# Decoder step on one core: sample states on 96 rows, ten tiles of the second output unit in the norm's banks, fourteen cache copies moved

## The chip, the cores and the metric

The program runs on one core of a Trainium2 chip. The metric is the device time of one execution in microseconds. TensorE (PE) multiplies matrices, VectorE (DVE) and ScalarE (ACT) work on tiles, GpSimd (POOL) adds and issues some transfers, SyncE (SP) issues most transfers. The eight banks of the accumulator memory have the names bSA, bSB, bO, bZ, bT0, bT1, bPA and bPB; the profile writes bT for bT0 and bT1.

## The reference, cut to what matters

One layer of a decoder serves a prompt of 512 tokens and 8 samples of 4 new tokens, 544 columns in all, with a model width of 2048. One input projection feeds gated linear attention (4 heads, key width 128, value width 256) and dilated softmax attention (8 heads, with a cache of 2048 positions for each sample). An output projection, a residual, a norm and a convolutional feed-forward part follow. Among the outputs are each sample's new linear-attention state and its shifted cache.

```python
# linear attention, block by block; a sample's four tokens are one block
s_new = s * exp(tot)[..., None] + einsum('bhsd,bhsv->bhdv', k_to_end, v)
# cache of a sample: old rows shifted by the four new ones
k_buf = concatenate([cache_k, k_new], axis=1)[:, -2048:]
# output projection and residual
h = x + concatenate([o_a, o_b], axis=-1) @ w_out
```

## The kernel before, in words

All matrices are kept transposed: features on the 128 rows, the 544 tokens on columns, in two halves of 272. Work on TensorE comes in *units*: 128 columns of a weight matrix against all 16 feature tiles of the input. A float32 weight is split by ScalarE into a rounded high part (`hi`, line 1043) and by VectorE into the rest (`lo`, line 1423), the input likewise, and `mm3` (lines 626 to 628) adds three fp32r products per tile and half. A unit is so 96 products of 272 columns. Two weight buffers take turns. `project(x, c)` does one half of unit c in bank bPA or bPB; it waits until both parts of the weights are there (`lo_done`) and until VectorE has read the bank's last result (`half_read`).

The engines run in their own program order and meet at semaphores. The stages are: softmax attention of 8 heads (to about 462 us), linear attention of 4 heads (to about 803), output projection of 16 units (to about 997), feed-forward. Units of the next head are projected between the steps of the present one.

**A linear-attention head** (`gla_head`, three times in a loop and once written out) turns keys and values into rows (ScalarE copies them from the banks: `KN`, `GVN`), adds up the chunk states, makes the outputs, and updates the 8 samples' states. For that update VectorE multiplies the 32 sample rows of the values by a 0/1 mask per sample (`masked(i)`, line 1601, four samples at a time, twice a head), and TensorE multiplies the keys with each masked copy in float32 (`sample_adds(i)`, line 911, four products of 256 columns, once ahead of the norm's sums in line 916 and once later). VectorE adds the result to the decayed states (line 1645). The norm over a head's 256 values goes through banks bZ and bT0: TensorE sums squares into them, VectorE reads them (lines 1650, 1651), ScalarE takes a root, VectorE inverts (line 1654) and multiplies (lines 1661 to 1665) into the last tiles of the residual.

**The output projection.** In the last head the first output unit starts early: `first_out` works its tiles in the order 8 to 15, then 0 to 7, both halves at a time. The two tiles that the last head makes come last (`READY` = 14), when `mixed_high` (line 1108) and `mixed_low` (line 1556) have split them. The second unit follows with `project`, then a loop of seven rounds does two units each. Behind each unit VectorE adds the residual (line 1692), ScalarE squares and scales (lines 1192, 1194) and splits the weights of the unit after the next, and GpSimd stores the tile (line 2113).

**SP's queue** in the looped heads holds, behind each of six weight loads, two or three copies of the samples' value cache (`copy_cache`, 584 KB each). In the output stage it holds, for each of twelve units, a weight load, a residual tile (as soon as the store that uses its buffer has landed) and three or four copies of the key cache. Ahead of the fourth unit's load it waits for the last head's sample states to be stored.

Of the kernel before, what the change touches and what calls it, by code (L numbers as in the profile page):

```python
# [15 lines left out]
F32 = mybir.dt.float32  # L16
# [78 lines left out]
def build(nc, A, O):  # L95
# [57 lines left out]
    SMK, o = place("causal_sample", [SAMP, SAMP], F32, o)  # L153
    RM, o = place("row_of_sample", [SAMP, NB], F32, o)

# [31 lines left out]
    ET, o = place("decay_total", [P, 16], F32, o)  # L187
    VM, o = place("v_masked", [SAMP, 4, DV], F32, o)
    OS, o = place("outputs_sample", [P, 2, SAMP], F32, o)
    assert o <= o_reset  # L190
    AT = KD
    OR = KD


# [97 lines left out]
    or_done, or_turned, os_done = sem("or_done"), sem("or_turned"), sem("os_done")  # L292
    vm_done, us_done, ss_done = sem("vm_done"), sem("us_done"), sem("ss_done")
    sq2_done, gsum_done, gms_done, gsqrt_done = sem("sq2_done"), sem("gsum_done"), sem("gms_done"), sem("gsqrt_done")
# [85 lines left out]
    H, ACTS = (nc.dram_tensor(n, s, F32, kind="Internal").ap() for n, s in (("hidden", [KT, P, T]), ("activations", [FT, P, T])))  # L380
    MIX_ORDER, READY = [*range(8, KT), *range(8)], KT - 2
    POFF = [0, 128, 384, 768]
# [5 lines left out]
    def _(sp):  # L388
# [87 lines left out]
        for it in range(GH - 1):  # L476
            cols = [it * P + (C_QA + P), it * P + (C_KA + P), it * DV + (C_VA + DV),
                    it * DV + (C_VA + DV + P), it * DV + (C_GA + DV), it * DV + (C_GA + DV + P)]
            j = 0
            for i, col in enumerate(cols):  # L480
                load_unit(unit_of(col), flat, U_GLA + 6 + i, it, 6)
                for _ in range(3 if i < 2 else 2):
                    copy_cache(1, it, j)
                    j += 1
            assert j == COPIES

# [19 lines left out]
        for it in range(3):  # L506
            for i in range(4):
                load_unit(w_cols(w_out, it * 4 * P + (3 + i) * P), raw3, U_OUT + 3 + i, it, 4)
                load_x(it * 4 + (2 + i), 2 + i, it)
                for j in range([0, 4, 8, 11][i], [4, 8, 11, 14][i]):  # L510
                    copy_cache(0, it, j)
        load_unit(w_cols(w_out, 15 * P), raw3, U_OUT + 15)
# [110 lines left out]
    def _(pe):  # L623
# [12 lines left out]
        def steps(x, c, lo, hi, it=None, k=0):  # L636

            if lo == 0 and x == 0:
                pe.wait_ge(lo_done, at(c + 1, it, k))
            if lo == 0 and c >= 1:  # L640
                pe.wait_ge(half_read, at(2 * c + x - 1, it, 2 * k))
            s = c % 2
            for kt in range(lo, hi):
                w = slice(kt * P, (kt + 1) * P)
                t = slice(x * HALF, (x + 1) * HALF)
                ins = mm3(PJ[x][:, 0:HALF], WH[s][:, w], WL[s][:, w], XH[:, kt, t], XL[:, kt, t], kt == 0, kt == KT - 1)
            if hi == KT:
                ins.then_inc(half_done, 1)
# [170 lines left out]
        def gla_head(it, c, last):  # L819
# [28 lines left out]
            pe.wait_ge(ke_done, n(1, 1))  # L848
            pe.wait_ge(gv_done, n(4, 2))
            for j in range(4):  # L850
                turn(T0[:, j * P:(j + 1) * P], g0[:, 1, j * P:(j + 1) * P], P)
            turn(T1[0:SAMP, 0:P], g0[:, 1, SEQ:T], P).then_inc(kn_turned, 1)
            project(1, u + 1, it, 6)
            pe.wait_ge(kn_done, n(2, 2))
            pe.wait_ge(half_read, at(2 * u + 2, it, 12))
            turn_v(g1[:, 0])
            project(0, u + 2, it, 6)

            pe.wait_ge(gv_done, n(4, 4))
            for ch in range(NCH):  # L860
# [46 lines left out]
            def sample_adds(i):  # L907
                pe.wait_ge(vm_done, n(2, i + 1))
                for b in range(4):
                    dst = [T1, BO][b // 2]  # L910
                    ins = pe.matmul(dst[:, (b % 2) * DV:(b % 2 + 1) * DV], KN[0:SAMP, 4, :], VM[:, b, :], start=True, stop=True)
                ins.then_inc(us_done, 1)
# [18 lines left out]


        first_out(READY, KT)
        project(0, U_OUT + 1)
        project(1, U_OUT + 1)
        for it in range(7):
            for i in range(2):
                project(0, U_OUT + 2 + i, it, 2)
                project(1, U_OUT + 2 + i, it, 2)

# [92 lines left out]
    def _(act):  # L1033
# [76 lines left out]
        def gla_head(it, c, last):  # L1110
# [25 lines left out]
            def v_rows(w):  # L1136
                act.wait_ge(gv_turned, n(2, w + 1))
                dv = slice(w * P, (w + 1) * P)
                act.activation(GVN[:, 0:4, dv], BO[:, :].rearrange("p (j d) -> p j d", j=4), ACT.Copy).then_inc(gv_done, 1)
                act.activation(GVN[0:SAMP, 4, dv], T1[0:SAMP, 0:P], ACT.Copy).then_inc(gv_done, 1)  # L1140
            v_rows(0)
            hi(u + 2, it, 6)
            act.wait_ge(kn_turned, n(1, 1))
            act.activation(KN[:, 0:4, :], T0[:, :].rearrange("p (j d) -> p j d", j=4), ACT.Copy).then_inc(kn_done, 1)
            act.activation(KN[0:SAMP, 4, :], T1[0:SAMP, 0:P], ACT.Copy).then_inc(kn_done, 1)
            v_rows(1)
# [33 lines left out]
        def out_step(c, it=None, k=0, nxt=True):  # L1180
# [12 lines left out]
            g = GF[:, m:m + 1] if it is None else GF[:, bass.ds(it * k + m, 1)]  # L1193
            act.activation(hb(m if it is None else it * k + m), XR[m % 2][:, :], ACT.Copy, scale=g).then_inc(scaled, 1)
        out_step(U_OUT)
        out_step(U_OUT + 1)
        for it in range(6):
# [219 lines left out]
    def _(dve):  # L1417
# [140 lines left out]
        def gla_head(it, c, last):  # L1558
# [38 lines left out]

            def masked(i):

                for b in range(4):  # L1600
                    ins = dve.tensor_scalar(VM[:, b, :], GVN[0:SAMP, 4, :], RM[:, 4 * i + b:4 * i + b + 1], None, ALU.mult)
                ins.then_inc(vm_done, 1)
            dve.wait_ge(gv_done, n(4, 4))
            masked(0)
            read_half(g1[:, 1], 1, 1.0, u + 1, it, 6)
# [45 lines left out]
            dve.tensor_scalar(EB[:, SEQ:T], T0[:, 0:SAMP], 1.0 / DV, EPS, ALU.mult, ALU.add).then_inc(gms_done, 1)  # L1651
            masked(1)
            dve.wait_ge(gsqrt_done, n(1, 1))
# [27 lines left out]
        def out_step(c, it=None, k=0, nxt=True):  # L1681
            m = c - U_OUT
            if m and nxt:
                lo(c + 1, it, k)
            for x in range(2):
                if x == 0:
                    dve.wait_ge(xr_in[m % 2], at(16 * (m // 2 + 1), it, 8 * k))
                    if m == 0:
                        dve.wait_ge(mh_done, KT)
                dve.wait_ge(half_done, at(2 * c + x + 1, it, 2 * k))  # L1690
                t = slice(x * HALF, (x + 1) * HALF)
                dve.tensor_tensor(XR[m % 2][:, t], PJ[x][:, 0:HALF], XR[m % 2][:, t], ALU.add).then_inc(half_read, 1)

# [546 lines left out]
def _constants():  # L2240
# [17 lines left out]
        "sample_mask": ((r[:, None] // NQ == r[None, :] // NQ) & (r[:, None] <= r[None, :])).astype(np.float32),  # L2258
        "row_mask": (r[:, None] // NQ == np.arange(NB)[None, :]).astype(np.float32),
        "pick": (p[:, None] % SAMP == np.arange(RANK)[None, :]).astype(np.float32),  # L2260
# [60 lines left out]
```

## Time and profile before

| | |
|---|---|
| median of 3 runs | 2455.87 us (2455.42 to 2456.04) |
| profiled execution | 2455.66 us, span 2453.7 us |
| PE busy | 2393.7 us (98%) |
| DVE busy | 1672.5 us (68%) |
| ACT busy | 1033.8 us (42%) |
| POOL busy | 580.7 us (24%) |
| moved by DMA | 492.67 MB, mean 201 GB/s |

The span is the profiled execution without what lies around it on the device. A busy share is an average over stages; which wait counts is read from the stage. A start time in a timeline is us from the span's start. Matmuls overlap, so the pace is the distance between two starts, not a duration. A float32 product appears as two records. PEclk 1.00 stands for the clock of 2.4 GHz, 0.50 for 1.2 GHz.

### The profile page before, as it was taken

How to read it: one execution, taken by the hardware profiler on the slowest of the kernel's cores; microseconds unless marked ns; L12 is line 12 of the kernel's file. 1: busy time of each engine (PE TensorE's matmuls, PEld its weight loads, DVE VectorE, ACT ScalarE, POOL GpSimd, SP SyncE). 2: the span in 40 equal slices, each digit the busy share in tenths (PEclk: the TensorE clock that was granted, in tenths of full speed). 3: DMA queues.
4: the chain of work that ended last, by engine and by line, in shares of the span. 5: the costliest groups of instructions: out<-in, count | busy, mean ns of one | idle time of the engine just before them, and what ended most of it. 6: DMA issues, size and time to landing. Idle time of an engine off the chain costs nothing.

```text
span 2453.7 us, 46359 instructions
## 1 busy us (share of the span) xinstructions
PE 2393.7 (98%) x19540; PEld 2326.7 (95%) x19540; DVE 1672.5 (68%) x2257; ACT 1033.8 (42%) x1377; POOL 580.7 (24%) x710
## 2 busy tenths in 40 slices
PE   8999999999999899799999999999999999999996
PEld 7988999999999899799999999999999999999995
DVE  7333333343544434888888888888888888888876
ACT  5222122223324222455555555555555535565553
POOL 0000010000000111134444443444444402222222
PEclk9999999999999999999999999999999999999998
DMA  6556666444543698446666666666666766777663
GB/s 256 221 218 250 235 234 222 175 180 180 198 184 99 221 294 275 110 139 217 207 218 215 227 216 225 217 205 206 206 217 207 259 183 158 190 182 178 152 150 105
DMA packets 332206, 492.67 MB, mean 201 GB/s; under 512 B 16032, under 2 KB 301280, under 8 KB 317920
## 3 DMA queue, kind: packets, MB, share of 16 engines
q1 hardware_dynamic: 299008, 429.51, 52.1%
q0 software_dynamic: 32992, 60.21, 10.4%
q8 instruction: 154, 2.52, 0.4%
q14 instruction: 52, 0.43, 0.1%
HBM read 436.24 MB, written 165.11 MB: 245 GB/s over the span
## 4 chain that ended last, share of the span: by engine, by line
PE 92%; DVE 3%; DMA 1%; ACT 1%; POOL 1%; issue 1%; SPq 0%; DVEq 0%; POOLq 0%; ACTq 0%
PE bPA L626 5%; PE bPB L626 5%; PE bPA L628 5%; PE bPB L627 5%; PE bPA L627 5%; PE bPB L628 5%; PE bSB L956 4%; PE bSB L957 4%; PE bSB L955 4%; PE bSA L956 3%; PE bSA L957 3%; PE bSA L955 3%; PE bZ L956 2%; PE bZ L955 2%; PE bT L956 2%; PE bZ L957 2%
## 5 line engine op out<-in xcount | busy, mean ns | idle before, releaser
L626 PE MATMUL bPA<-x_high,w_high 128*128 128x272 f32 x992 | 296.5, 299 | 8.7 <-DVE x_low L1556 7.0
L626 PE MATMUL bPB<-x_high,w_high 128*128 128x272 f32 x992 | 289.2, 292 | 0.0
L627 PE MATMUL bPB<-x_low,w_high 128*128 128x272 f32 x992 | 286.8, 289 | 0.0
L628 PE MATMUL bPA<-x_high,w_low 128*128 128x272 f32 x992 | 286.7, 289 | 0.0
L628 PE MATMUL bPB<-x_high,w_low 128*128 128x272 f32 x992 | 286.2, 289 | 0.0
L627 PE MATMUL bPA<-x_low,w_high 128*128 128x272 f32 x992 | 286.1, 288 | 0.0
L1423 DVE TENSOR_TENSOR w_low<-w_raw,w_high 128x2048 fp32r<-128x2048 f32 x63 | 151.2, 2400 | 134.1 <-ACT w_high L1043 134.1
L1715 DVE TENSOR_TENSOR w_low<-up_raw,w_high 128x1024 fp32r<-128x1024 f32 x154 | 187.8, 1220 | 54.8 <-ACT w_high L1213 54.8
L1715 DVE TENSOR_TENSOR w_low<-w_raw,w_high 128x1024 fp32r<-128x1024 f32 x154 | 188.3, 1222 | 51.8 <-ACT w_high L1213 51.8
L955 PE MATMUL bSA<-form_high,w_high 128*128 128x272 f32 x704 | 204.3, 290 | 9.7 <-DVE residual_low L1786 7.5
L955 PE MATMUL bSB<-form_high,w_high 128*128 128x272 f32 x704 | 203.8, 289 | 6.9 <-ACT sum L1221 6.9
L1213 ACT ACTIVATE w_high<-w_raw 128x1024 fp32r<-128x1024 f32 x154 | 160.3, 1055 | 116.0 <-DVE w_raw L1728 101.6
L1213 ACT ACTIVATE w_high<-up_raw 128x1024 fp32r<-128x1024 f32 x154 | 160.4, 1054 | 113.4 <-DVE up_raw L1728 99.8
L626 PEld LDWEIGHTS bPA<-x_high,w_high 128*128 128x128 f32 x992 | 187.6, 189 | 21.1 <-issue 12.4
L957 PE MATMUL bSA<-form_high,w_low 128*128 128x272 f32 x704 | 204.4, 290 | 0.0
L957 PE MATMUL bSB<-form_high,w_low 128*128 128x272 f32 x704 | 204.0, 290 | 0.0
L626 PEld LDWEIGHTS bPB<-x_high,w_high 128*128 128x128 f32 x992 | 187.5, 189 | 8.9 <-issue 8.6
L627 PEld LDWEIGHTS bPA<-x_low,w_high 128*128 128x128 f32 x992 | 187.8, 189 | 1.9 <-issue 1.9
L627 PEld LDWEIGHTS bPB<-x_low,w_high 128*128 128x128 f32 x992 | 187.5, 189 | 0.0
L628 PEld LDWEIGHTS bPA<-x_high,w_low 128*128 128x128 f32 x992 | 187.4, 189 | 0.0
L628 PEld LDWEIGHTS bPB<-x_high,w_low 128*128 128x128 f32 x992 | 187.3, 189 | 0.0
L2202 POOL DMA_DIRECT2D residual<-part x80 | 96.2, 1202 | 346.3 <-ACT part L1328 319.1
(475 smaller groups left out, 7517.7 us busy)
## 6 DMA issues: line engine op xcount, KB each, us to landing
out_v_sample<-in_cache_swa_v SPq DMA_DIRECT2D x112, 584.0 KB, 8.1
out_k_sample<-in_cache_swa_k SPq DMA_DIRECT2D x112, 584.0 KB, 7.9
w_raw<-in_w_in_units SPq DMA_DIRECT2D x47, 1024.0 KB, 5.1
up_raw<-in_w_up SPq DMA_DIRECT2D x44, 1024.0 KB, 7.8
w_raw<-in_w_up SPq DMA_DIRECT2D x44, 1024.0 KB, 8.9
cache_set<-in_k_sets SPq DMA_DIRECT2D x16, 1792.0 KB, 9.0
cache_set<-in_v_sets SPq DMA_DIRECT2D x16, 1792.0 KB, 7.5
up_raw<-in_w_down SPq DMA_DIRECT2D x24, 1024.0 KB, 7.5
```

Of the source, the lines that this page charges most:

```text
L626: pe.matmul(out, w_h, x_h, start=first, stop=False)
L627: pe.matmul(out, w_h, x_l, start=False, stop=False)
L628: return pe.matmul(out, w_l, x_h, start=False, stop=last)
L955: pe.matmul(into[:, 0:HALF], ring(WH, n)[:, w], HI[i][:, k, :], start=k == 0 and i in (0, 1, 5), stop=False, skip_group_check=True)
L956: pe.matmul(into[:, 0:HALF], ring(WH, n)[:, w], LO[i][:, k, :], start=False, stop=False, skip_group_check=True)
L957: ins = pe.matmul(into[:, 0:HALF], ring(WL, n)[:, w], HI[i][:, k, :], start=False, stop=k == HK - 1, skip_group_check=True)
L1213: act.activation(ring(WH, n), weight_block(qc % 2, *BLOCK_OF[i]), ACT.Copy).then_inc(wf_hi, 1)
L1423: dve.tensor_tensor(WL[c % 2][:, :], RAW[c % 2][:, :], WH[c % 2][:, :].bitcast(F32), ALU.subtract).then_inc(lo_done, 1)
L1715: dve.tensor_tensor(ring(WL, n), weight_block(qc % 2, *BLOCK_OF[i]), ring(WH, n).bitcast(F32), ALU.subtract).then_inc(wf_lo, 1)
L2202: pool.dma_start(out_block(d, s, t), PARTS[j][:, :, :], accum_op=ALU.add).then_inc(parts_in[j], 16)
```

## The change

The sample states: ScalarE copies the sample rows of keys and values into strips of 32 rows in fp32r, and VectorE makes the remainders, so that 96 rows hold (high, high, rest) of the keys and (high, rest, high) of the values. The mask goes to the keys, for all eight samples in one instruction. One fp32r product over 96 rows then gives what a float32 product over 32 rows gave. The second output unit: its first ten tiles are worked in banks bZ and bT0 behind the last head, ahead of the first unit's last two tiles; the other six follow them. VectorE reads that unit from those banks, the third unit no longer waits for it, ScalarE splits the third unit's weights ahead of the first unit's squares, and the loop of the output units is written out. Fourteen copies of the key cache go out in the looped heads (five, five, four), one behind each of the first weight loads; the output stage keeps 28, two or three a unit.

```diff
-    VM, o = place("v_masked", [SAMP, 4, DV], F32, o)
+    KM, o = place("k_masked", [3 * SAMP, NB, DK], F32R, o)
+    KS, _ = place("k_parts", [3 * SAMP, DK], F32R, o_la + 4 * DK * 4)
+    VS, r = place("v_parts", [3 * SAMP, DV], F32R, o_scr + 2 * T * 4)
+    KR, r = place("k_rows", [SAMP, DK], F32, r)
+    PART0, PART1, PART2 = (slice(i * SAMP, (i + 1) * SAMP) for i in range(3))
-    MIX_ORDER, READY = [*range(8, KT), *range(8)], KT - 2
+    MIX_ORDER, READY, FILL = [*range(8, KT), *range(8)], KT - 2, 10
+    SECOND = (BZ, T0)
...
+                if i < 5 and it * 5 + i < COPIES:
+                    copy_cache(0, 0, it * 5 + i)
...
-                for j in range([0, 4, 8, 11][i], [4, 8, 11, 14][i]):
-                    copy_cache(0, it, j)
+                for n in range(28 * (4 * it + i) // 12, 28 * (4 * it + i + 1) // 12):
+                    copy_cache(0, 1 + n // COPIES, n % COPIES)
...
-                pe.wait_ge(half_read, at(2 * c + x - 1, it, 2 * k))
+                pe.wait_ge(half_read, 2 * c + x - 3 if it is None and c == U_OUT + 2 else at(2 * c + x - 1, it, 2 * k))
...
             def sample_adds(i):
-                pe.wait_ge(vm_done, n(2, i + 1))
+                pe.wait_ge(km_done, n(2, 2))
...
-                    ins = pe.matmul(dst[:, (b % 2) * DV:(b % 2 + 1) * DV], KN[0:SAMP, 4, :], VM[:, b, :], start=True, stop=True)
+                    ins = pe.matmul(dst[:, (b % 2) * DV:(b % 2 + 1) * DV], KM[:, 4 * i + b, :], VS[:, :], start=True, stop=True)
...
+        def second_out(lo, hi):
+            both_halves(SECOND, U_OUT + 1, MIX_ORDER, XH, XL, ml_done, lo, hi, half_done)
+        pe.wait_ge(lo_done, U_OUT + 2)
+        pe.wait_ge(gms_done, 2 * GH)
+        second_out(0, FILL)
         first_out(READY, KT)
-        project(0, U_OUT + 1)
-        project(1, U_OUT + 1)
-        for it in range(7):
-            for i in range(2):
-                project(0, U_OUT + 2 + i, it, 2)
-                project(1, U_OUT + 2 + i, it, 2)
+        second_out(FILL, KT)
+        for c in range(U_OUT + 2, U_OUT + KT):
+            project(0, c)
+            project(1, c)
...
+                act.activation(VS[PART0, dv], T1[0:SAMP, 0:P], ACT.Copy).then_inc(gv_done, 1)
+                act.activation(VS[PART2, dv], T1[0:SAMP, 0:P], ACT.Copy).then_inc(gv_done, 1)
...
-            act.activation(KN[0:SAMP, 4, :], T1[0:SAMP, 0:P], ACT.Copy).then_inc(kn_done, 1)
+            act.activation(KR[:, :], T1[0:SAMP, 0:P], ACT.Copy).then_inc(kn_done, 1)
+            act.activation(KS[PART0, :], T1[0:SAMP, 0:P], ACT.Copy).then_inc(kn_done, 1)
+            act.activation(KS[PART1, :], T1[0:SAMP, 0:P], ACT.Copy).then_inc(kn_done, 1)
...
+        hi(U_OUT + 2)
         out_step(U_OUT)
-        out_step(U_OUT + 1)
+        out_step(U_OUT + 1, nxt=False)
...
-                for b in range(4):
-                    ins = dve.tensor_scalar(VM[:, b, :], GVN[0:SAMP, 4, :], RM[:, 4 * i + b:4 * i + b + 1], None, ALU.mult)
-                ins.then_inc(vm_done, 1)
-            dve.wait_ge(gv_done, n(4, 4))
-            masked(0)
+            dve.wait_ge(kn_done, n(4, 4))
+            own.mark(dve.tensor_tensor(KS[PART2, :], KR[:, :], KS[PART0, :].bitcast(F32), ALU.subtract))
+            own.wait()
+            dve.tensor_tensor(KM[:, :, :], KS[:, :].bitcast(F32).unsqueeze(1).broadcast_to([3 * SAMP, NB, DK]),
+                              RM[:, :].unsqueeze(2).broadcast_to([3 * SAMP, NB, DK]), ALU.mult).then_inc(km_done, 1)
+            dve.wait_ge(gv_done, n(8, 8))
+            dve.tensor_tensor(VS[PART1, :], GVN[0:SAMP, 4, :], VS[PART0, :].bitcast(F32), ALU.subtract).then_inc(km_done, 1)
...
-            masked(1)
             dve.wait_ge(gsqrt_done, n(1, 1))
...
+                out = SECOND if it is None and m == 1 else PJ
+                dve.tensor_tensor(XR[m % 2][:, t], out[x][:, 0:HALF], XR[m % 2][:, t], ALU.add).then_inc(half_read, 1)
```

TensorE at the end of the last head, before: the second group of sample products, then tile 14 of the first output unit (w_high_53 is its weight buffer, w_high_56 the second unit's).

```order
L911 MATMUL bT<-v_masked,k_to_end_rows 128x256 x2
L911 MATMUL bO<-v_masked,k_to_end_rows 128x256 x2
L626 MATMUL bPA<-x_high,w_high_53 128x272
L627 MATMUL bPA<-x_low,w_high_53 128x272
L628 MATMUL bPA<-x_high,w_low_54 128x272
```

The same place in the change. The six rows on w_high_56 are one tile of the second unit; ten such tiles stand here before the first row on w_high_53.

```order
L919 MATMUL bT<-v_parts,k_masked 128x256 x2
L919 MATMUL bO<-v_parts,k_masked 128x256 x2
L634 MATMUL bZ<-x_high,w_high_56 128x272
L635 MATMUL bZ<-x_low,w_high_56 128x272
L636 MATMUL bZ<-x_high,w_low_57 128x272
L634 MATMUL bT<-x_high,w_high_56 128x272
L635 MATMUL bT<-x_low,w_high_56 128x272
L636 MATMUL bT<-x_high,w_low_57 128x272
...
L634 MATMUL bPA<-x_high,w_high_53 128x272
```

So 60 products moved ahead of tile 14; the count of products is the same.

ScalarE behind the split of the last two mixed tiles, before (squares and residual belong to the first output unit, w_high_53 to the third):

```order
L1108 ACTIVATE x_high<-residual 128x544 x2
L1192 ACTIVATE squares<-x_again_127 128x544
L1194 ACTIVATE residual<-x_again_127,g_ffn 128x544
L1043 ACTIVATE w_high_53<-w_raw_52 128x2048
L1192 ACTIVATE squares<-x_again_128 128x544
```

And in the change:

```order
L1120 ACTIVATE x_high<-residual 128x544 x2
L1055 ACTIVATE w_high_53<-w_raw_52 128x2048
L1208 ACTIVATE squares<-x_again_130 128x544
L1210 ACTIVATE residual<-x_again_130,g_ffn 128x544
L1208 ACTIVATE squares<-x_again_131 128x544
```

The weight copy of the third unit moved ahead of the first unit's squares.

## Rows read from the trace of the kernel before

**Rows 1.** The page's busy time of TensorE; the waits of TensorE (total us, times, longest)

```profile
PE 2393.7 (98%) x19540; PEld 2326.7 (95%) x19540; DVE 1672.5 (68%) x2257; ACT 1033.8 (42%) x1377; POOL 580.7 (24%) x710
...
PE bPA L626 <- DVE x_low L1556: 7.0, 1, 7.0
```

**Rows 2.** Timeline of TensorE, last head: start, us, instruction, [idle before <- releaser]

```profile
803.58 1.10 PE L911 MATMUL bT<-v_masked,k_to_end_rows 32*128 32x256 f32 x4 [0.46 <-DVE v_masked L1601]
...
812.56 0.60 PE L626 MATMUL bPA<-x_high,w_high 128*128 128x272 f32 x1 [7.02 <-DVE x_low L1556]
```

**Rows 3.** Timeline of VectorE, last head and first output units

```profile
802.22 0.18 DVE L1651 TENSOR_SCALAR tmp_b<-bT 128x32 f32<-128x32 f32 x1
802.32 1.12 DVE L1601 TENSOR_SCALAR v_masked<-gla_v_rows,row_of_sample 32x256 f32<-32x256 f32 x4
803.37 3.53 DVE L1654 RECIPROCAL tmp_b<-tmp_b 128x544 f32<-128x544 f32 x1
...
811.79 1.35 DVE L1556 TENSOR_TENSOR x_low<-residual,x_high 128x544 fp32r<-128x544 f32 x2
...
821.16 2.29 DVE L1423 TENSOR_TENSOR w_low<-w_raw,w_high 128x2048 fp32r<-128x2048 f32 x1 [5.04 <-ACT w_high L1043]
```

**Rows 4.** Table of stretches: us, PE, PEld, DVE, ACT, POOL busy, PEclk, DMA, GB/s

```profile
808.00:809.00 1.00, 0.00 (x0) 0.00 (x0) 0.96 (x2) 0.00 (x0) 0.00 (x0) 0.57 0.00 0
818.00:819.00 1.00, 1.00 (x9) 1.00 (x8) 0.00 (x0) 0.97 (x2) 0.00 (x0) 0.81 0.06 14
1018.00:1019.00 1.00, 1.00 (x10) 1.00 (x9) 1.00 (x2) 1.00 (x2) 0.00 (x0) 1.00 0.00 0
```

**Rows 5.** Timeline of TensorE, second looped head, around both groups of sample products

```profile
617.92 1.13 PE L911 MATMUL bT<-v_masked,k_to_end_rows 32*128 32x256 f32 x4
...
619.84 1.13 PE L916 MATMUL bZ<-tmp_a,ones 128*128 128x512 f32 x2
...
626.95 0.29 PE L628 MATMUL bPA<-x_high,w_low 128*128 128x272 f32 x1
...
629.32 0.29 PE L627 MATMUL bPB<-x_low,w_high 128*128 128x272 f32 x1
```

**Rows 6.** Timeline of TensorE, first product of the third and the fourth output unit

```profile
829.04 0.29 PE L626 MATMUL bPA<-x_high,w_high 128*128 128x272 f32 x1
...
841.07 0.29 PE L626 MATMUL bPA<-x_high,w_high 128*128 128x272 f32 x1
```

**Rows 7.** Timeline of VectorE and TensorE, second looped head: unit u+5

```profile
630.13 2.28 DVE L1423 TENSOR_TENSOR w_low<-w_raw,w_high 128x2048 fp32r<-128x2048 f32 x1
...
635.20 0.29 PE L626 MATMUL bPA<-x_high,w_high 128*128 128x272 f32 x1
```

**Rows 8.** Timeline of ScalarE, last head and first output unit

```profile
802.43 0.66 ACT L1170 ACTIVATE tmp_b<-tmp_b 128x544 f32<-128x544 f32 x1 [3.32 <-DVE tmp_b L1651]
...
819.23 1.90 ACT L1043 ACTIVATE w_high<-w_raw 128x2048 fp32r<-128x2048 f32 x1
```

**Rows 9.** Timeline of ScalarE, last head, copies of the value rows

```profile
768.15 0.60 ACT L1139 ACTIVATE gla_v_rows<-bO 128x512 f32<-128x512 f32 x1 [5.82 <-PE bT L678]
768.65 0.25 ACT L1140 ACTIVATE gla_v_rows<-bT 32x128 f32<-32x128 f32 x1
```

**Rows 10.** Timeline of TensorE, feed-forward start

```profile
1017.36 0.36 PE L955 MATMUL bSA<-form_high,w_high 128*128 128x272 f32 x1 [2.27 <-issue]
```

**Rows 11.** DMA view: loads issued at 818.9 and 828.4 (us to landing last); queues, 829 to 960

```profile
w_raw<-in_w_out SPq DMA_DIRECT2D x1, 1024.0 KB, 6.0
...
w_raw<-in_w_out SPq DMA_DIRECT2D x1, 1024.0 KB, 12.1
...
q8 instruction: 8, 0.13, 0.4%
```

**Rows 12.** Timeline of SP and ScalarE, second looped head: a load and its use

```profile
567.23 0.33 SPq L400 DMA_DIRECT2D w_raw<-in_w_in_units  x1
...
585.41 1.90 ACT L1043 ACTIVATE w_high<-w_raw 128x2048 fp32r<-128x2048 f32 x1
```

More of the change, by code:

```diff
@@ L153, in build @@
     SMK, o = place("causal_sample", [SAMP, SAMP], F32, o)
-    RM, o = place("row_of_sample", [SAMP, NB], F32, o)
+    RM, o = place("row_of_sample", [3 * SAMP, NB], F32, o)
     PTS, r = place("probs_sample_t", [P, KB + 1, 4, 8], F32, o_sp)
@@ L192, in build @@
     OR = KD
+    KS, _ = place("k_parts", [3 * SAMP, DK], F32R, o_la + 4 * DK * 4)
+    VS, r = place("v_parts", [3 * SAMP, DV], F32R, o_scr + 2 * T * 4)
+    KR, r = place("k_rows", [SAMP, DK], F32, r)
+    assert r <= o_scr + 3 * T * 4
+    PART0, PART1, PART2 = (slice(i * SAMP, (i + 1) * SAMP) for i in range(3))
     BLOCK = HK * HALF * 4
@@ L292, in build @@
     or_done, or_turned, os_done = sem("or_done"), sem("or_turned"), sem("os_done")
-    vm_done, us_done, ss_done = sem("vm_done"), sem("us_done"), sem("ss_done")
+    km_done, us_done, ss_done = sem("km_done"), sem("us_done"), sem("ss_done")
     sq2_done, gsum_done, gms_done, gsqrt_done = sem("sq2_done"), sem("gsum_done"), sem("gms_done"), sem("gsqrt_done")
@@ L848, in gla_head @@
             pe.wait_ge(ke_done, n(1, 1))
-            pe.wait_ge(gv_done, n(4, 2))
+            pe.wait_ge(gv_done, n(8, 4))
             for j in range(4):
@@ L853, in gla_head @@
             project(1, u + 1, it, 6)
-            pe.wait_ge(kn_done, n(2, 2))
+            pe.wait_ge(kn_done, n(4, 4))
             pe.wait_ge(half_read, at(2 * u + 2, it, 12))
@@ L857, in gla_head @@
             project(0, u + 2, it, 6)
-            pe.wait_ge(gv_done, n(4, 4))
+            pe.wait_ge(gv_done, n(8, 8))
             for ch in range(NCH):
@@ L1596, in gla_head @@
             read_half(g1[:, 1], 0, 1.0, u + 1, it, 6)
-            def masked(i):
-                for b in range(4):
-                    ins = dve.tensor_scalar(VM[:, b, :], GVN[0:SAMP, 4, :], RM[:, 4 * i + b:4 * i + b + 1], None, ALU.mult)
-                ins.then_inc(vm_done, 1)
-            dve.wait_ge(gv_done, n(4, 4))
-            masked(0)
+            dve.wait_ge(kn_done, n(4, 4))
[5 more added lines that the diff above has]
+            dve.tensor_tensor(VS[PART1, :], GVN[0:SAMP, 4, :], VS[PART0, :].bitcast(F32), ALU.subtract).then_inc(km_done, 1)
             read_half(g1[:, 1], 1, 1.0, u + 1, it, 6)
@@ L1691, in out_step @@
                 t = slice(x * HALF, (x + 1) * HALF)
-                dve.tensor_tensor(XR[m % 2][:, t], PJ[x][:, 0:HALF], XR[m % 2][:, t], ALU.add).then_inc(half_read, 1)
+                out = SECOND if it is None and m == 1 else PJ
+                dve.tensor_tensor(XR[m % 2][:, t], out[x][:, 0:HALF], XR[m % 2][:, t], ALU.add).then_inc(half_read, 1)
         def differences(k, it=None, per=0):
@@ L2258, in _constants @@
         "sample_mask": ((r[:, None] // NQ == r[None, :] // NQ) & (r[:, None] <= r[None, :])).astype(np.float32),
-        "row_mask": (r[:, None] // NQ == np.arange(NB)[None, :]).astype(np.float32),
+        "row_mask": np.tile((r[:, None] // NQ == np.arange(NB)[None, :]).astype(np.float32), (3, 1)),
         "pick": (p[:, None] % SAMP == np.arange(RANK)[None, :]).astype(np.float32),
```

## The prediction

> **What bounds the kernel now.** I read the page first: TensorE is busy 98% of the span [rows 1]. So the question is how much of its own work goes away, and how much of its idle time. The chain of waits, cut down to TensorE, answers the second part: in the stretch that the change touches one wait counts, 7.02 us in front of the first output unit's last two tiles, until VectorE has made x_low of them [rows 1]. The timeline of TensorE shows what stands around that hole [rows 2], that of VectorE what ends it [rows 3], and a table of short stretches what the clock did [rows 4]. TensorE stopped at 805.5 (812.56 less 7.02); the granted clock averaged 0.57 in the microsecond from 808, so it fell to 0.50 near 808.1, and it averaged 0.81 from 818, so it came back near 818.4. The hole costs more than its length.
>
> **Part 1, sample products on 96 rows.** Before, a group of four f32 products of 256 columns (line 911) is issued from 617.92 to 619.84, in 1.92 us [rows 5]. The new group is four fp32r products of one pass each. The nearest row for their price is the unit pace: 96 fp32r products of 272 columns from 829.04 to 841.07 [rows 6], 0.1253 us each. I take 0.125, so 0.50 a group, and 1.42 saved. The Trainium skill's page "TensorE: Matmul & The Clock Gate", in "Back-to-back issue gap", gives a warm gap of columns over 2.4 GHz plus 2.5 ns: an estimate of 0.109 us for 256 columns and 0.116 for 272. Here 272 columns take 0.125, so the row decides; by the rule a group would be 0.06 us cheaper, 0.4 us over six groups.
>
> The second group of a head stands between fp32r products. From the last one before it to the second one behind it is 2.37 us [rows 5]; in six steps of 0.125 it is 0.75, so 1.62 is saved. The first group still has the f32 norm sums behind it and keeps one switch of format. That is 3.04 us a head, **9.1 us for heads 0 to 2**. Bounds: a product costs at least the row's pace cut to 256 columns (0.118, another 0.2 us in all), and at most what f32 costs now, 0.48 each, which saves nothing.
>
> What is late next in these heads is the weight pair of unit u+5: VectorE's subtraction starts at 630.13, TensorE begins the unit at 635.20 [rows 7], and a subtraction takes 2.29 [rows 3], so 2.8 us are to spare. TensorE comes 3.04 earlier. If VectorE gained nothing, 0.3 us a head would come back; but the sample products reach it 1.4 us sooner, and four masks leave its path, so I take no stall.
>
> The operands cost other engines time. ScalarE gets six copies of 32x128 a head; one lasts 0.25 and follows its neighbour by some 0.15, so about 0.9 us, behind an idle time of 5.82 [rows 9]. VectorE gets three instructions for eight masks; its 96x1024 product costs about half a 128x2048 subtraction, 1.15 us [rows 3], and stands where the first four masks were. I cost both at nothing, since both engines wait for TensorE there; without that cover they would be some 2 us a head.
>
> **Part 2, ten tiles into the hole.** The fill needs the norm's banks, whose second read ends at 802.40 [rows 3]. In the last head the first sample group ends 1.4 us sooner, so TensorE has done tiles 6 to 13 and the second group by then. The fill starts at 802.46 and takes 60 x 0.1253 = 7.5 us, to 810.0. VectorE's path to the last x_low gets shorter by only 0.24: its masks started at 802.32 and its reciprocal at 803.37 [rows 3], which can now start when ScalarE's root ends, at 803.09 [rows 8]. So tile 14 starts at 812.32 in place of 812.56, and **about 2.3 us stay idle**.
>
> Does the clock fall in them? It fell 2.6 us after TensorE stopped [rows 2, 4]. A wait of 2.27 us before 1017.36 [rows 10] is followed by a microsecond at 1.00 with ten products [rows 4]. I take no fall. Then tiles 14 and 15 (12 products) end at 813.8, and the second unit's other 36 products at 818.33. The third unit's weights come out the same: the first unit's bank is done at 814.0, ScalarE's copy takes 1.90 [rows 8], VectorE's subtraction 2.29 [rows 3], 818.3. That copy now stands ahead of the squares, which wait for the sample states' store. So the third unit starts at 818.4 where it started at 829.04 [rows 6]: **10.6 us**. In it are 7.02 less 2.3 of idle time, 2.6 for the slow clock (26 products from 812.56 to 818.4 take 5.8 us, at full pace 3.3), the last head's 3.0 of sample products, and 0.3 of the wait for the masks before 803.58 [rows 2].
>
> Behind it TensorE paces every unit, 12.03 us [rows 6]. What is late next is the fourth unit's load, which SP issues after that store, near 818.6. One without copies beside it landed in 6.0 us [rows 11], so at 824.6; 4.2 us of splitting make 828.9, against 830.5 when TensorE needs it. The fifth is issued near 827 behind two copies. Behind four it took 12.1 us [rows 11]; I take 9, and it is ready at 840.2 against 842.5. At 12.1 it would stall 0.8 us.
>
> **Part 3, fourteen copies, and the straight loop.** Fourteen issues of SP move from the output stage to the three looped heads. There a load goes out at 567.23 and is used at 585.41 [rows 12], 18 us later, where the slowest landing shown is 12.1 [rows 11]. The output stage's transfers get room, but TensorE waits for none of them. Zero both ways; bounds: the 0.8 above, and up to 1 us gained if a load for the feed-forward part lands sooner. The loop of the output units, written out, saves nothing: two units follow each other at 12.03 without a gap.
>
> **Sum.** 9.1 + 10.6 = 19.7 us off the profiled execution (2455.66 us, its span 2453.7; 0.2 below the median of 2455.87): **2436.0 us**.
>
> **Rivals.**
> - *The clock falls in the rest of the hole.* For it: the old fall came after 2.6 us, barely more than 2.3. Against it: rows 10 with the last of rows 4. The slow stretch returns: 2.6 us, 2438.6. [...]
> - *The fourth or fifth unit's weights come late.* SP's queue does not move with TensorE, since the sample states' store holds it. It decides from landings over 7.6 and 11.2 us. Price 1 to 4 us: 2437 to 2440.
> - *The narrow products gain nothing.* If four of them take 1.92 us as now, part 1 is lost, and the fill ends up to 1 us later: about 2446.
> - *The change doesn't fill the hole,* because the banks or the order make TensorE wait as before: part 1 alone, 2446.5. Against it: the banks are free at 802.4.
> - *Slower: TensorE waits for instructions in the straight code.* The 14 units behind the fill were a loop run seven times. 131 us of that stage show 8 packets of instructions [rows 11], one in 16.4 us, so some 10 in the 168 us of 14 units. If each held TensorE for the 2.27 us that rows 10 put down to issue, 23 us are lost: 2459. From 2.0 us a packet on it eats the whole gain. Against it: the loop fetched as much, and no gap shows between its rounds.
>
> **How the numbers follow.** The forecast has 0.62; the clock 0.13; late weights 0.11; narrow products without gain 0.05; no fill 0.04; instruction waits 0.03; anything else 0.02. The range starts at 2433.5: the forecast less the cheapest product (0.2), an earlier load (1), and the rest of the hole being partly closed. It ends at 2444, past the clock and late weights together (2442.6), and leaves out the last four cases. Within 0.2% (4.9 us, about what a measurement can tell from no change) only mishaps that add up end: 0.03. Slower by more: 0.03, the instruction waits. Faster: 0.94.
>
> **What would show it.** Right: groups at the new line 919 of 0.5 us; about 2.3 us idle before tile 14, at clock 1.00; the third unit starting 19 to 20 us before 829.04; later units still 12.03 apart; the feed-forward part's holes as long as before. Wrong: four products over 1 us, clock 0.50 near 805 (the old 814), or TensorE waiting for w_low of the third to fifth unit, or for issue, in the output stage.

## The result and the profile after

The change took the median from 2455.95 us (2455.42 to 2456.37, 4 runs) to 2436.02 us (2435.76 to 2436.98, 4 runs): ratio 0.992, 95% interval 0.9907 to 0.9933. The forecast was 2436.0. The profiled execution of the changed kernel took 2435.99 us, its span 2434.2.

The page and the waits of TensorE up to the feed-forward part's start, of the changed kernel, against [rows 1]:

```profile
PE 2378.4 (98%) x19508; PEld 2316.2 (95%) x19508; DVE 1669.1 (69%) x2237; ACT 1040.4 (43%) x1401; POOL 581.3 (24%) x710
```

```profile
PE bSA L967 <- DVE residual_low L1803: 7.8, 2, 7.0
PE bPA L634 <- DVE x_low L1573: 2.0, 1, 2.0
PE bT L919 <- DVE states_sample L1662: 0.3, 1, 0.3
```

TensorE works 15.3 us less (2393.7 to 2378.4) and the wait for x_low went from 7.02 to 2.04, 5.0 less. That makes 20.3, where the span is 19.5 shorter; the feed-forward part's start gave some back (below).

Timeline of TensorE in the second looped head of the changed kernel, around both groups of sample products (start, us, instruction), against [rows 5]:

```profile
614.54 0.29 PE L636 MATMUL bPB<-x_high,w_low 128*128 128x272 f32 x1
614.66 0.40 PE L919 MATMUL bT<-v_parts,k_masked 96*128 96x256 f32 x2
614.90 0.40 PE L919 MATMUL bO<-v_parts,k_masked 96*128 96x256 f32 x2
615.14 1.02 PE L924 MATMUL bZ<-tmp_a,ones 128*128 128x512 f32 x2
616.00 0.30 PE L925 MATMUL bT<-tmp_a,ones 128*128 128x32 f32 x2
...
622.15 0.29 PE L636 MATMUL bPA<-x_high,w_low 128*128 128x272 f32 x1
622.28 0.41 PE L919 MATMUL bT<-v_parts,k_masked 96*128 96x256 f32 x2
622.53 0.40 PE L919 MATMUL bO<-v_parts,k_masked 96*128 96x256 f32 x2
622.76 0.29 PE L634 MATMUL bPB<-x_high,w_high 128*128 128x272 f32 x1
622.89 0.29 PE L635 MATMUL bPB<-x_low,w_high 128*128 128x272 f32 x1
```

A group of four products takes 0.48 us where it took 1.92. From the last fp32r product before the second group to the second one behind it is 0.74 where it was 2.37.

Timeline of TensorE at the end of the last head of the changed kernel, and the first products of the third and fourth output unit; against [rows 2, 6]:

```profile
792.13 0.50 PE L919 MATMUL bT<-v_parts,k_masked 96*128 96x256 f32 x2 [0.26 <-DVE states_sample L1662]
792.47 0.40 PE L919 MATMUL bO<-v_parts,k_masked 96*128 96x256 f32 x2
792.88 0.36 PE L634 MATMUL bZ<-x_high,w_high 128*128 128x272 f32 x1
...
800.39 0.29 PE L636 MATMUL bT<-x_high,w_low 128*128 128x272 f32 x1
802.72 0.39 PE L634 MATMUL bPA<-x_high,w_high 128*128 128x272 f32 x1 [2.04 <-DVE x_low L1573]
...
808.89 0.39 PE L634 MATMUL bPA<-x_high,w_high 128*128 128x272 f32 x1
...
821.05 0.29 PE L634 MATMUL bPA<-x_high,w_high 128*128 128x272 f32 x1
```

Table of stretches of the changed kernel (columns as in [rows 4]); the clock stays at 1.00, 2.4 GHz, through the rest of the hole:

```profile
801.00:802.00 1.00, 0.00 (x0) 0.00 (x0) 1.00 (x4) 0.78 (x2) 0.00 (x0) 1.00 0.00 0
802.00:803.00 1.00, 0.28 (x2) 0.28 (x3) 1.00 (x3) 0.00 (x0) 0.37 (x1) 1.00 0.00 0
803.00:804.00 1.00, 1.00 (x10) 1.00 (x10) 0.30 (x1) 0.00 (x0) 0.52 (x1) 1.00 0.87 218
```

Timelines of VectorE, ScalarE and SP of the changed kernel: the third unit's weights, and the fifth's from load to use; against [rows 3, 8]:

```profile
806.55 2.29 DVE L1440 TENSOR_TENSOR w_low<-w_raw,w_high 128x2048 fp32r<-128x2048 f32 x1 [1.50 <-ACT w_high L1055]
...
829.27 2.29 DVE L1440 TENSOR_TENSOR w_low<-w_raw,w_high 128x2048 fp32r<-128x2048 f32 x1 [7.57 <-ACT w_high L1055]
```

```profile
804.60 1.92 ACT L1055 ACTIVATE w_high<-w_raw 128x2048 fp32r<-128x2048 f32 x1 [2.81 <-PE bPB L636]
...
827.32 1.92 ACT L1055 ACTIVATE w_high<-w_raw 128x2048 fp32r<-128x2048 f32 x1 [4.29 <-DMA w_raw<-in_w_out]
```

```profile
816.26 2.27 SPq L420 DMA_DIRECT2D out_k_sample<-in_cache_swa_k  x2
818.57 0.58 SPq L406 DMA_DIRECT2D w_raw<-in_w_out  x1
```

The third unit's weights are ready at 808.84 (806.55 and 2.29) and TensorE begins it at 808.89 with no gap: its own work and the weights end together. The fifth unit's are ready at 831.56; TensorE begins that unit at 833.09.

The feed-forward part's start, against [rows 10]: the first hole before, then both holes of the changed kernel and the clock behind the second.

```profile
1004.27 0.57 PE L955 MATMUL bSA<-form_high,w_high 128*128 128x272 f32 x1 [6.60 <-DVE residual_low L1786]
```

```profile
984.63 0.56 PE L967 MATMUL bSA<-form_high,w_high 128*128 128x272 f32 x1 [6.98 <-DVE residual_low L1803]
...
997.72 0.36 PE L967 MATMUL bSA<-form_high,w_high 128*128 128x272 f32 x1 [2.58 <-issue]
```

```profile
998.00:999.00 1.00, 1.00 (x10) 1.00 (x9) 1.00 (x2) 1.00 (x2) 0.00 (x0) 1.00 0.00 0
```

The output stage ends 20.02 us earlier and the feed-forward part starts 19.64 us earlier: 0.4 us are given back there.

### The profile page after: what moved, and what is told of

The parts are those of the page before. It is cut to its first block, busy times and chain, and to the rows that moved or that the text cites. A ratio compares the mean times of both kernels' runs of the same rounds, so it can differ in the third digit from the quotient of the medians.

```text
span 2434.2 us, 46299 instructions
## 1 busy us (share of the span) xinstructions
PE 2378.4 (98%) x19508; PEld 2316.2 (95%) x19508; DVE 1669.1 (69%) x2237; ACT 1040.4 (43%) x1401; POOL 581.3 (24%) x710
## 4 chain that ended last, share of the span: by engine, by line
PE 92%; DVE 3%; DMA 1%; ACT 1%; POOL 1%; issue 1%; SPq 0%; DVEq 0%; POOLq 0%; ACTq 0%
PE bPA L634 5%; PE bPB L634 5%; PE bPB L635 5%; PE bPA L636 5%; PE bPB L636 5%; PE bPA L635 5%; PE bSB L968 4%; PE bSB L969 4%; PE bSB L967 4%; PE bSA L968 3%; PE bSA L969 3%; PE bSA L967 3%; PE bZ L968 2%; PE bZ L967 2%; PE bT L968 2%; PE bZ L969 2%
## 5 line engine op out<-in xcount | busy, mean ns | idle before, releaser
L634 PE MATMUL bPA<-x_high,w_high 128*128 128x272 f32 x976 | 290.9, 298 | 3.7 <-DVE x_low L1573 2.0
L634 PE MATMUL bPB<-x_high,w_high 128*128 128x272 f32 x976 | 284.1, 291 | 0.0
L635 PE MATMUL bPB<-x_low,w_high 128*128 128x272 f32 x976 | 281.9, 289 | 0.0
L636 PE MATMUL bPA<-x_high,w_low 128*128 128x272 f32 x976 | 281.6, 289 | 0.0
L636 PE MATMUL bPB<-x_high,w_low 128*128 128x272 f32 x976 | 281.3, 288 | 0.0
L635 PE MATMUL bPA<-x_low,w_high 128*128 128x272 f32 x976 | 280.6, 288 | 0.0
```

The lines of the kernel that those rows point to most:

```text
L634: pe.matmul(out, w_h, x_h, start=first, stop=False)
L635: pe.matmul(out, w_h, x_l, start=False, stop=False)
L636: return pe.matmul(out, w_l, x_h, start=False, stop=last)
```

## The experiments

Executions of one kernel differ by 1 to 4 us, so each trace is also read by stages, each from one instruction to another of the same trace: *heads 0 to 2*, from the gate product (bT<-gate_rank,w_gate) of the first linear-attention head to that of the last; *last head and output*, from there to the first feed-forward product behind its first hole; and what lies before and behind. The last head's gate product, before and in the change:

```profile
739.73 1.09 PE L829 MATMUL bT<-gate_rank,w_gate 16*128 16x512 f32 x2 [0.62 <-DVE proj L1438]
```

```profile
730.08 1.09 PE L837 MATMUL bT<-gate_rank,w_gate 16*128 16x512 f32 x2 [0.63 <-DVE proj L1455]
```

| trace | starts at | heads 0 to 2 | last head, output | feed-forward |
|---|---|---|---|---|
| before | 464.61 | 275.12 | 264.54 | 1449.4 |
| the change | 464.71 | 265.37 | 254.55 | 1449.6 |
| e1 products alone | 465.50 | 265.38 | 263.69 | 1450.4 |
| e2 fill alone | 466.01 | 275.11 | 256.43 | 1449.5 |
| e3 copies alone | 465.44 | 275.10 | 262.99 | 1449.0 |
| e4 without copies | 465.09 | 265.43 | 259.36 | 1450.1 |
| e5 four tiles | 465.75 | 265.37 | 260.50 | 1450.1 |
| e6 thirteen tiles | 465.56 | 265.44 | 256.27 | 1450.5 |
| e7 early split | 466.12 | 265.39 | 253.19 | 1450.5 |
| e8 the change again | 464.96 | 265.36 | 254.47 | 1449.6 |
| e9 early split again | 464.84 | 265.41 | 252.73 | 1452.1 |

The kernels' edits touch neither the time before the first head nor the feed-forward part, and yet the one moves by 1.5 us and the other by 3 (for the second see e9).

**e1, the sample products alone.** The diff's KM, KS, VS lines on the kernel before; output stage and copies as before:

```diff
-                    ins = pe.matmul(dst[:, (b % 2) * DV:(b % 2 + 1) * DV], KN[0:SAMP, 4, :], VM[:, b, :], start=True, stop=True)
+                    ins = pe.matmul(dst[:, (b % 2) * DV:(b % 2 + 1) * DV], KM[:, 4 * i + b, :], VS[:, :], start=True, stop=True)
```

> The kernel before with part 1 alone (stacked sample products; no fill, copies as before). My theory: each of the three looped heads is shorter by the 3.25 us that stand between two heads' gate products in the changed kernel's trace (91.7 before, 88.45 after), 9.75 in all; in the last head VectorE's path sets the end, so there only the 0.24 us of the masks count: 2455.95 - 10.0 = 2446.0 us, and the hole in front of tile 14 gets longer, to 7.02 + 2.9 = 9.9 us less the 0.24. Rival, that every sample product saved counts wherever it stands: four heads, 13 us, 2443.0.

Measured: 2446.83 us (2446.38 to 2447.81), ratio 0.9966 (0.9953 to 0.9979). The three looped heads are 9.74 us shorter; the last head's gain went into a longer wait for x_low, 9.85 us in place of 7.02:

```profile
803.52 0.59 PE L631 MATMUL bPA<-x_high,w_high 128*128 128x272 f32 x1 [9.85 <-DVE x_low L1565]
```

So part 1 takes 9.7 us out of the heads by itself, and the last head's 3 us count only together with the fill. The rival, 2443.0, is out. (The stage behind is 0.85 us shorter as well, although its hole is longer: the clock came back 3.2 us behind this hole, where it took 5.8 before.)

**e2, the fill alone.** Part 2 on the kernel before, with the f32 sample products and the copies where they were:

```diff
+        second_out(0, FILL)
         first_out(READY, KT)
-        project(0, U_OUT + 1)
-        project(1, U_OUT + 1)
+        second_out(FILL, KT)
```

> The kernel before with part 2 alone (ten tiles of the second unit in the norm's banks; sample products in float32 as before). My theory: the second float32 group ends at 805.5, the fill of 7.5 us ends at 813.0, later than the last x_low, so no idle time is left before tile 14 and the clock stays at 1.00; the third unit starts near 819.1 in place of 829.04: 2455.95 - 10.0 = 2446.0 us. The parts then add up to the whole (19.9). Rival, that the rest of the hole or the weights of the third unit decide: 2 to 3 us less gained, 2448 to 2449.

Measured: 2448.51 us (2447.78 to 2450.48), ratio 0.9973 (0.9964 to 0.9983), the rival's number, but not for the rival's reason. No wait for x_low is left, but the stage is only 8.1 us shorter. Its timeline of TensorE and its table of stretches show why:

```profile
804.97 1.10 PE L912 MATMUL bT<-v_masked,k_to_end_rows 32*128 32x256 f32 x4 [0.45 <-DVE v_masked L1607]
...
806.86 0.39 PE L627 MATMUL bZ<-x_high,w_high 128*128 128x272 f32 x1
...
807.92 0.43 PE L628 MATMUL bZ<-x_low,w_high 128*128 128x272 f32 x1
808.15 0.43 PE L629 MATMUL bZ<-x_high,w_low 128*128 128x272 f32 x1
```

```profile
807.00:808.00 1.00, 1.00 (x8) 1.00 (x9) 1.00 (x1) 0.00 (x0) 0.00 (x0) 0.87 0.09 16
808.00:809.00 1.00, 1.00 (x6) 1.00 (x6) 0.96 (x3) 0.00 (x0) 0.00 (x0) 0.50 0.00 0
...
811.00:812.00 1.00, 1.00 (x9) 1.00 (x8) 1.00 (x2) 0.19 (x1) 0.00 (x0) 0.92 0.00 0
```

The clock fell to 0.50, 1.2 GHz, while TensorE was at work, some 0.9 us behind the f32 group and its pause of 0.45 us. It stayed low for about 3.4 us, in which 15 products began where 27 would have: about 1.5 us that the fill earned and the clock took. With the 96-row products the clock did not fall there in any of the six traces with ten tiles or more in the hole. The fourth unit took 12.43 us in place of 12.04, since the fifth unit's weights came late (the copies had not moved): 0.4 more.

**e3, the copies alone.** Fourteen copies moved, nothing else:

```diff
+                if i < 5 and it * 5 + i < COPIES:
+                    copy_cache(0, 0, it * 5 + i)
```

> The kernel before with part 3 alone (fourteen copies moved to the looped heads). My theory: no TensorE wait ends earlier or later, 2455.9 us, within 0.5. Rival, that the output stage gains from fewer transfers: 2454 or less; rival that the heads' loads get late: 2457 or more.

Measured: 2455.76 us (2454.45 to 2456.28), ratio 1.0 (0.999 to 1.0009): no effect on the kernel before. Its profiled execution is 1.3 us under that median, with the same 7.02 us wait and a stage of 262.99. TensorE stopped there at 806.35 (813.37 less 7.02), and the clock fell then, not 2.6 us later as before, and so came back sooner behind the hole (a mean of 0.68 over the microsecond in which it fell):

```profile
806.00:807.00 1.00, 0.35 (x2) 0.00 (x0) 1.00 (x1) 0.00 (x0) 0.00 (x0) 0.68 0.00 0
```

**e4, the change without the moved copies.** All 42 copies in the output stage:

```diff
-                for n in range(28 * (4 * it + i) // 12, 28 * (4 * it + i + 1) // 12):
-                    copy_cache(0, 1 + n // COPIES, n % COPIES)
+                for j in range([0, 4, 8, 11][i], [4, 8, 11, 14][i]):
+                    copy_cache(0, it, j)
```

> The changed kernel with the fourteen copies back in the output stage (parts 1 and 2 alone). Theory A, the copies cost and protect nothing: 2436.0 us. Theory B, the fifth output unit's weights had only 1.5 us to spare in the changed kernel (its load goes out at 818.57 behind two copies and lands 8.7 us later; the split ends at 831.56, TensorE needs it at 833.09): with four copies ahead the load goes out 1 to 2 us later and lands some 12 us after that, so TensorE waits 2 to 4 us for w_low of the fifth unit, 2438 to 2440 us.

Measured: 2439.36 us (2438.72 to 2441.86), ratio 0.9937 (0.9922 to 0.9952): 3.3 us over the change (2.1 over its second set, e8), as theory B has it. The trace is of the slowest of its executions. Its SP, ScalarE and TensorE timelines show the fifth unit:

```profile
816.74 3.83 SPq L420 DMA_DIRECT2D out_k_sample<-in_cache_swa_k  x4
820.61 1.28 SPq L406 DMA_DIRECT2D w_raw<-in_w_out  x1
```

```profile
832.11 1.91 ACT L1053 ACTIVATE w_high<-w_raw 128x2048 fp32r<-128x2048 f32 x1 [8.67 <-DMA w_raw<-in_w_out]
```

```profile
836.85 0.57 PE L632 MATMUL bPA<-x_high,w_high 128*128 128x272 f32 x1 [3.19 <-DVE x_again L1707]
```

The load goes out 3.87 us behind the first of four copies (816.74 to 820.61), in the change 2.31 behind the first of two: 1.6 us later. It is used 11.5 us after its issue, where the change needs 8.75. TensorE waits 3.19 us for VectorE's read of its bank, which stands in VectorE's order behind the weight subtraction, and the clock falls: this unit takes 13.41 us in place of 12.03. So the copies gain nothing by themselves and protect what the fill gains. The count of copies alone does not set how long they hold the queue; what else does was not tried. In the kernel before, four took 2.41 us:

```profile
825.99 2.41 SPq L414 DMA_DIRECT2D out_k_sample<-in_cache_swa_k  x4
```

**e5, four tiles in the hole; e6, thirteen.**

```diff
-    MIX_ORDER, READY, FILL = [*range(8, KT), *range(8)], KT - 2, 10
+    MIX_ORDER, READY, FILL = [*range(8, KT), *range(8)], KT - 2, 4
```

> The changed kernel with 4 tiles of the second unit ahead of tile 14 in place of 10. The fill ends 4.5 us earlier, the idle time before tile 14 grows from 2.0 to some 6.5 us. Theory, that a hole of this length drops the clock as before and the next 26 products go at half pace: 4.5 + 2.6 = 7.1 us more, 2443.1 us, with a granted clock of 0.50 in the table of stretches behind 802.7. Rival, that only the idle time counts: 2440.5 us.

> The changed kernel with 13 tiles ahead of tile 14. TensorE has no idle time left before tile 14 (less than 0.3 us), but the third unit's weights are split only when the first unit is done. Theory, that this split sets the third unit's start as much as TensorE's own work does (both ended at 808.8 to 808.9 in the changed kernel): same time, 2436.0 us within 0.5, and a new wait of TensorE of some 2.3 us for VectorE's w_low before the third unit. Rival, that the idle time is TensorE's to save: 2433.7 us.

Measured: e5 2443.67 us (2443.17 to 2444.34), ratio 0.9949 (0.9934 to 0.9963), near the theory. The wait for x_low is 6.59 us, the clock 0.50 behind it. But the stage is 5.95 us longer, not 7.1: 4.55 are the wait, so the clock cost 1.4 us and not 2.6. It came back about 3.0 us behind the hole. That the sum came out near 2443.1 is in part chance: 1.5 us more lie before the first head and in the feed-forward part.

e6 2439.69 us (2438.7 to 2441.44), ratio 0.9933 (0.9917 to 0.995), where 2436.0 was expected. The wait for w_low came with the size expected, 2.13 us, and the third unit starts as in the change against the last head's start (78.82 us behind its gate product; 78.81). The rest of the stage is 1.7 us longer. The timeline of TensorE and the table of stretches of e6:

```profile
809.82 0.60 PE L634 MATMUL bPA<-x_high,w_high 128*128 128x272 f32 x1 [2.13 <-DVE w_low L1440]
```

```profile
809.00:810.00 1.00, 0.18 (x1) 0.18 (x2) 1.00 (x2) 0.93 (x2) 0.00 (x0) 0.88 0.03 7
810.00:811.00 1.00, 1.00 (x5) 1.00 (x6) 0.47 (x2) 0.37 (x1) 0.04 (x1) 0.50 0.63 174
```

The clock fell after a wait of 2.13 us, near 809.8, just as TensorE took up work again. It had not after 2.04 us in the change. The third unit took 13.62 us in place of 12.16. That was the rival of a falling clock, met by another wait of the same length. Of the 3.6 us by which this execution (2439.62 us) is over the change's, the rest lies before the first head (0.85) and in the feed-forward part (0.9), which the edit does not touch.

**e7 and e9, the third unit's weights split early; e8, the change again.** Thirteen tiles fill the hole and both halves of the limit at 808.8 go: ScalarE copies fourteen of the sixteen pieces of the third unit's weights during the fill, VectorE subtracts them behind the last x_low. SP's loads move as well: the fourth unit's goes out ahead of the wait for the sample states' store, each later one a place earlier in the queue.

```diff
+        load_unit(w_cols(w_out, 3 * P), raw3, U_OUT + 3)
         sp.wait_ge(ss_done, 2 * GH)
...
+        act.wait_ge(early_lo, 2)
+        for a, b in ((8 * P, KT * P), (0, 6 * P)):
+            act.activation(WH[0][:, a:b], RAW[0][:, a:b], ACT.Copy).then_inc(early_hi, 1)
...
-        hi(U_OUT + 2)
+        act.activation(WH[0][:, 6 * P:8 * P], RAW[0][:, 6 * P:8 * P], ACT.Copy).then_inc(hi_done, 1)
```

> The changed kernel with 13 tiles ahead of tile 14, and the third unit's weights split early: ScalarE copies 14 of its 16 tiles in its idle time behind the norm's root, when the first unit's ready tiles are done, VectorE subtracts them behind the last x_low, and only two tiles wait for the first unit's end; SP issues the fourth unit's load ahead of its wait for the sample states' store, and the later loads ahead of the residual tile. Theory: the third unit starts when TensorE's products end, at 806.5 in place of 808.9, and the later loads keep up: 2433.7 us. Rival, that the split then waits on VectorE or a load comes late: 2436 us or more, with a TensorE wait for w_low of the third to fifth unit.

> The change itself once more, beside the early split of the third unit's weights on the same chip. If the 1 to 1.5 us by which traces differ ahead of the linear attention belong to the execution, its median is 2436 to 2437.5 here; if the earlier 2436.02 is the kernel's own, 2436.0 within 0.4.

> Theory A (the early split is shorter by what its stage showed, from the last head's gate product to the first feed-forward hole 253.2 us against 254.6, and the later start of its trace was the execution's): 1.4 us under the change on the same chip. Theory B (its moved loads cost at the program's start or elsewhere what they gain here): within 0.5 us of the change or above it.

Measured: e7 2437.75 us (2436.38 to 2438.65), ratio 0.9924 (0.9909 to 0.9939). On one chip, e8 2437.30 us (2436.22 to 2437.79) and e9 2436.91 us (2434.45 to 2438.21), ratios 0.9925 (0.9911 to 0.9938) and 0.9922 (0.9909 to 0.9934): not told apart. The change's own median moved by 1.3 us between two sets of runs, so differences of that size are the execution's.

The stage itself is shorter in both traces of the early split, 253.19 and 252.73 us against 254.55 and 254.47, so theory A is right about the stage and wrong about the whole. The third unit starts 76.5 us behind the gate product in both, where the change has 78.8, as expected; but it takes 12.75 us in e7 and 12.35 in e9, not 12.16. The rest of the gain goes where the edit touches nothing: in e7 before the first head (1.4 us against the change) and in the feed-forward part (0.9), in e9 all in the feed-forward part (2.5 against e8).

The first feed-forward product behind a short wait at 1955, in e8 and in e9:

```profile
1956.39 0.36 PE L634 MATMUL bPA<-act_high,w_high 128*128 128x272 f32 x1 [1.59 <-DVE residual L1888]
```

```profile
1955.55 0.46 PE L634 MATMUL bPA<-act_high,w_high 128*128 128x272 f32 x1 [1.79 <-DVE residual L1901]
```

Tables of stretches there and behind the hole that ends near 1026, in e8 and in e9:

```profile
1030.00:1031.00 1.00, 1.00 (x7) 1.00 (x6) 1.00 (x2) 0.00 (x0) 0.00 (x0) 0.64 0.05 16
...
1956.00:1957.00 1.00, 0.60 (x5) 0.64 (x6) 1.00 (x4) 0.98 (x1) 0.00 (x0) 1.00 0.27 88
```

```profile
1030.00:1031.00 1.00, 1.00 (x8) 1.00 (x6) 0.96 (x2) 0.05 (x1) 0.00 (x0) 0.67 0.00 0
...
1955.00:1956.00 1.00, 0.45 (x2) 0.48 (x3) 1.00 (x4) 0.82 (x1) 0.00 (x0) 0.83 0.29 92
1956.00:1957.00 1.00, 1.00 (x7) 1.00 (x6) 1.00 (x4) 1.00 (x2) 0.00 (x0) 0.50 0.08 27
```

In e9 the clock fell behind 1.79 us; in e8 it stayed at 1.00. From that product to the one behind a wait near 2360 it is 404.65 us in e9 and 403.09 in e8.

Another 1.0 us is lost between the hole that ends at 1025 and this one (930.33 us against 929.36). That is mostly the clock too: low when that hole ends, it came back near 1030.7 in both, 5.4 us behind the hole's end in e9 (1025.22) and 3.7 in e8 (1027.03), and 1.8 us more at half the pace cost some 0.8 (an estimate from 0.23 us a product, as in e2 from 807.92 to 808.15, in place of 0.125). All eleven traces line up by this: the feed-forward part takes 1449.0 to 1449.6 us where 2.9 to 4.0 us of the low stretch lie behind that hole, and 1450.1 to 1450.5 where 5.0 to 6.0 do (e9 has its second fall on top). So a gain or loss of 1 us there does not by itself speak for or against an edit.

Whether the early split makes such losses likelier, or met them by chance, stays open: its fastest execution, 2434.45, is the fastest of all, its slowest above all of e8.

## Why the prediction was right

**Part 1** was right and a little small: 3.25 us a head (the heads' period went from 91.7 to 88.45), where 3.04 was the sum, so 9.75 for 9.1. The second group saves 1.63, as forecast (1.62). The first saves 1.53, not 1.42: a group takes 0.48, not 0.50, and 0.09 of the switch from fp32r in front of it (617.71 to 617.92 before, 614.54 to 614.66 now) is gone. The norm's first f32 sum takes 0.86 to the next in place of 0.96. Why was not tried; the remaining 0.09 of the 3.25 is about that. The operands' cost stayed covered: the mask of all samples took 1.22 us against an estimate of 1.15, and TensorE waits for none of the new tiles.

**Part 2** was right in its places as well as its sum. Shifted by the heads' 9.65 us (739.73 to 730.08), the fill was due at 792.81 and started at 792.88, tile 14 at 802.67 and started at 802.72, the third unit at 808.75 and started at 808.89. From the last head's gate product to the third unit it is 10.50 us shorter (89.31 to 78.81), for a forecast of 10.6. The idle rest was 2.04, not 2.3. One reading was off without harm: between 812.56 and 818.4 there are 24 products, not 26, so the slow stretch had cost 2.8 us, not 2.6; the sum goes by the third unit's start and does not use it. The clock did not fall, in the profiled execution and in e8; the reason given, that 2.27 us had not lowered it once, was no ground for certainty, as e6 and e9 show. The Trainium skill (page "TensorE: Matmul & The Clock Gate", section "HAM oscillation — how this bites in real kernels") tells of a kernel whose waits of some 3 to 5 us for transfers start every burst at the low clock. The waits of e6 and e9 were shorter than those, 2.13 and 1.79 us, and the clock fell all the same.

**Later units.** They stand 12.03 us apart. The fourth unit's weights were ready 1.6 us before their use, as forecast (the load was used 6.3 us after its issue, for 6.0), the fifth's 1.5 us, where 2.3 was forecast: behind two copies the load was used 8.75 us after its issue, for 9, but went out 1.2 us later than assumed; the two copies held SP for 2.27 us.

**Part 3** is zero against the kernel before, as e3 shows, but its bound was too small. *At 12.1 it would stall 0.8 us* is the step that failed: e4 waits 3.19 us and the clock adds 1.4. The sum had the landing about right (used 11.5 us after the issue, for 12.1) and the issue wrong: it goes out 2.8 us later than assumed, 1.2 as in the change and 1.6 more behind four copies. The rival of late weights had the place right, and its price of 1 to 4 us holds for the medians (3.3), not for this trace, the slowest execution (4.8 in the stage).

**The holes as long as before** was wrong by 0.4 us: 6.60 became 6.98. The sum hid it, because part 1 gave 0.65 more: the two stages give 9.75 and 9.99, and 0.25 is lost before and behind them. That the median lies 0.02 us from the forecast is luck; the same kernel's second set, e8, lies 1.3 above it.

**Rivals.** No wait for instructions stands in the output stage, and the narrow products gain what was forecast. The other two are real mechanisms of this kernel: the change passes the late weights by a margin of 1.5 us, and the falling clock without a margin that these runs could name.

## What to carry to other kernels

When a hole is filled, compute when the operand behind it is ready as well: here ten tiles make TensorE's work and the third unit's weights end together, and three more tiles only moved the wait. A change that gains on the critical path takes the slack of every load behind it, so the transfers in front of those loads may have to move with it, though moving them alone is worth nothing. And split a trace into stages between like instructions before a gain of 1 or 2 us is believed: the heads agreed to 0.1 us over eight traces while whole executions of one kernel differed by up to 4.

## What the runs showed of the hardware

- A short wait's length did not decide whether the clock fell. It stayed at 1.00 through waits of 2.04 and 2.58 us in the change and 1.59 us in e8, and fell with waits of 2.13 us in e6 and 1.79 us in e9. The falls of e6 and e9 cost 1.46 and 1.56 us.
- Nor did the fall have a fixed place: 2.6 us after TensorE stopped in the kernel before, as it stopped in e3, and as work began again in e6 and e9.
- In e2 it fell with TensorE busy for the whole microsecond, behind 1.9 us of f32 products on 32 rows and a pause of 0.45 us. Whether the products or the pause did it was not tried.
- In fp32r four products of 256 columns over 96 rows take 0.48 us, 0.12 each; in f32 over 32 rows 1.92, 0.48 each, four times as long.
- Equal copies held SP's queue for unequal times ahead of a weight load: two for 2.27 us in the change, four for 2.41 in the kernel before and for 3.83 in e4.
